# FFN front: first half of the tokens normalised in place and split first, four block products between the turns of the second half

## The chip, the cores and the metric

The kernel is one program on 1 core of a Trainium2 chip. The metric is device time in microseconds (us), median of several runs; one further execution was recorded by the hardware profiler.

## What is computed

One layer of an encoder trunk on 1024 tokens of width 1024 in float32: a half-step SwiGLU FFN, a mixer part (attention and a state space branch), a second half-step SwiGLU FFN, and a last RMSNorm. The change is in the FFN, which runs twice:

```python
h = h + FFN_RES * _swiglu(_rmsnorm(h, ffn1_norm[l]), ffn1_w_gate[l], ffn1_w_up[l], ffn1_w_down[l])
# _rmsnorm: x * lax.rsqrt(mean(x * x) + EPS) * g
# _swiglu:  (silu(x @ w_gate) * (x @ w_up)) @ w_down        D_MODEL 1024, D_FF 2816
```

## The kernel before

`ffn_phase` is called at L220 and L233 of the listing's builder (first FFN with `x` in DRAM, second FFN with the tokens already in the SBUF tensor `rows`). Its first part computes gate and up products as block products of the seven-product (Winograd) form. A "matrix" n is 256 columns of w_gate (n even) or w_up (n odd), 22 in all; its four 512x128 quarters A11..A22 and their sums S (four `sums(n)` instructions on POOL, L1109) are the stationary side, seven products q = 0..6 per matrix. The moving side B is the normalised tokens, turned to feature-by-token: seven blocks of 512 features by 512 tokens, q = 0 and 2 from the first 512 tokens alone (B11, B21), q = 6 from the second 512 alone (B22), q = 1, 3, 4, 5 from sums T of both. Each operand is split in a high and a low half (`hi` by ACT, `lo = src - hi` by DVE), and each product is 4 k-steps of three passes, 12 matmuls of 128x512 (L48 to L50).

The front, before the first product, does for pairs of token tiles i (tile i and tile i+4, 128 tokens each):

- SP loads the tiles of `x` (first FFN only), the gain `gb`, and w_gate's first matrix `raw0` (L780 to L786). The second FFN stores all of `rows` to DRAM in one transfer here (L788, 4 MB). w_up's first matrix `raw1` is loaded after the last turn (L789, L790).
- ACT squares each row (L844) with a sum, and takes the root (L379).
- DVE makes 1/sqrt with a five-step Newton chain (L92 to L96, 128x2 elements, each step waiting for the one before), and scales both tiles into a pair buffer (L961, `xn`, two buffers in turn).
- POOL makes the four sums T of the pair (L1092 to L1097), one buffer.
- PE turns the seven blocks of the pair, four 128x128 transposes each, into PSUM banks 0 to 6 (L1133). Block q of the next pair waits until DVE has read block q of the last (`s_blo`).
- ACT copies each bank to `B_hi` (L849), DVE subtracts it from the bank into `B_lo` (L968).

After four pairs the seven products of matrix 0 start, then matrix 1, and so on (`matrix`, L1141 to L1164). Per matrix the products go to three banks: product 0 to bank a, copied by ACT to `t1` (L879); product 1 to bank b, t2 = b + t1 by DVE (L1009); product 3 waits for t2; t3 after product 3 (L1016); then c22, c21, c12 (L1019 to L1024). ACT writes the next matrix's `A_hi` (L863) and DVE its `A_lo` (L944) for slot q once product q of the present matrix is done. At the start of an odd matrix ACT also applies Silu to three quarters of the gate result (L871), which needs product 6 of the matrix before. In the first FFN the engines carry a second job beside the products, the `Tables` of the state space branch, advanced by `tables_on(n, q)` in each slot: in slot (0,6) PE turns lam (L488) and ACT does an Exp (L524); in slots (1,0) and (1,2) PE turns c (L496), the second waiting for ACT's copy of the first (L530); in slot (1,0) DVE multiplies (L555).

The order on each engine is written by hand; the code of the front before:

```python
for i in range(QUAD):
    turn(i)
for j in range(2):
    matrix(0, j, True)
```

## Time and profile before

| what | value |
| --- | --- |
| median of 3 runs | 2445.79 us (2445.03 to 2451.75) |
| the profiled execution's own time | 2445.71 us |
| its span, first to last instruction | 2443.6 us |
| mean granted TensorE clock | 0.958 of full speed |
| PE, DVE, ACT, POOL busy | 91%, 52%, 35%, 24% of the span |
| front of the first FFN, to its first product | 0 to 58.22 us |
| front of the second FFN, rows complete to first product | 1721.9 to 1772.25 us |

Times inside the trace are microseconds from the span's start. An instruction's row has its start, its duration, engine, line, operation, written tile<-read tiles, shape and count; in square brackets the idle time of the engine before it and what ended it.

### The profile page before, as it was taken

What the parts mean: (1) busy time and instruction counts of PE and PEld (TensorE: products, weight loads), DVE (VectorE), ACT (ScalarE), POOL (GpSimd) and SP (SyncE); (2) the same over time, 40 slices, a digit from 0 to 9 for tenths busy, and PEclk for the clock granted to TensorE, in tenths of its full rate; (3) what the DMA queues carried; (4) which work ended last, traced back from release to release, by engine and by line L of the source; (5) the groups of instructions that cost most, each with busy time, mean ns of one, the idle gap of its engine ahead of it and who ended that gap; (6) DMA issues with size and microseconds to landing.
All of it is one profiled execution on the core that took longest, in us unless ns stands there. A gap on an engine that the chain in (4) does not pass through costs nothing. (4 is left out here: it accounts for less than half of the span.)

```text
span 2443.6 us, 27322 instructions
## 1 busy us (share of the span) xinstructions
PE 2227.4 (91%) x10338; PEld 1846.6 (76%) x10338; DVE 1281.9 (52%) x1944; ACT 863.9 (35%) x1396; POOL 582.6 (24%) x500
## 2 busy tenths in 40 slices
PE   3999999989996979998959998799599999999997
PEld 3878888878885878886837776577488888888886
DVE  7685555533435327952347777451755555543444
ACT  5423233322223233153137776321432323322232
POOL 4347777600000002220002221000533233310000
PEclk8999999999997999998979999899699999999999
DMA  2323232373112363322420000241222222246111
GB/s 100 101 91 102 89 112 97 101 285 103 48 35 93 114 104 131 102 78 71 127 73 6 4 6 1 95 177 39 95 87 92 81 87 69 90 182 224 50 53 67
DMA packets 169729, 223.63 MB, mean 92 GB/s; under 512 B 32064, under 2 KB 121664, under 8 KB 169088
## 3 DMA queue, kind: packets, MB, share of 16 engines
q1 hardware_dynamic: 169600, 221.90, 28.1%
q8 instruction: 83, 1.36, 0.2%
q14 instruction: 46, 0.38, 0.1%
HBM read 162.58 MB, written 59.28 MB: 91 GB/s over the span
## 5 line engine op out<-in xcount | busy, mean ns | idle before, releaser
L48 PE MATMUL psum<-f_B_hi,f_A_hi 128*128 128x512 f32 x1232 | 483.5, 392 | 1.4 <-ACT rows L879 1.1
L50 PE MATMUL psum<-f_B_hi,f_A_lo 128*128 128x512 f32 x1232 | 479.8, 389 | 0.0
L49 PE MATMUL psum<-f_B_lo,f_A_hi 128*128 128x512 f32 x1232 | 479.5, 389 | 0.0
L48 PE MATMUL psum<-f_wd_hi,f_hh 128*128 128x512 f32 x704 | 274.8, 390 | 8.0 <-DVE f_hh L979 8.0
L49 PE MATMUL psum<-f_wd_lo,f_hh 128*128 128x512 f32 x704 | 274.4, 390 | 0.0
L50 PE MATMUL psum<-f_wd_hi,f_hh 128*128 128x512 f32 x704 | 274.4, 390 | 0.0
L48 PEld LDWEIGHTS psum<-f_B_hi,f_A_hi 128*128 128x128 f32 x1232 | 231.3, 188 | 50.0 <-issue 2.8
L50 PEld LDWEIGHTS psum<-f_B_hi,f_A_lo 128*128 128x128 f32 x1232 | 231.2, 188 | 48.7
L49 PEld LDWEIGHTS psum<-f_B_lo,f_A_hi 128*128 128x128 f32 x1232 | 231.4, 188 | 46.9
L977 DVE TENSOR_TENSOR f_wd_lo<-f_wd_raw,f_wd_hi 128x1024 fp32r<-128x1024 f32 x88 | 107.8, 1225 | 301.0 <-ACT f_wd_hi L898 301.0
L898 ACT CAST f_wd_hi<-f_wd_raw 128x1024 fp32r<-128x1024 f32 x88 | 92.8, 1055 | 352.2 <-PE psum L50 324.1
L863 ACT CAST f_A_hi<-f_S 128x512 fp32r<-128x512 f32 x176 | 109.4, 623 | 302.6 <-PE psum L50 295.6
L1109 POOL TENSOR_TENSOR f_S<-f_raw 128x512 f32<-128x512 f32 x88 | 132.4, 1505 | 310.2 <-DVE f_A_lo L944 291.6
L944 DVE TENSOR_TENSOR f_A_lo<-f_raw,f_A_hi 128x512 fp32r<-128x512 f32 x128 | 125.1, 978 | 135.2 <-ACT f_A_hi L863 134.6
L48 PEld LDWEIGHTS psum<-f_wd_hi,f_hh 128*128 128x128 f32 x704 | 132.5, 188 | 36.3 <-issue 8.4
L50 PEld LDWEIGHTS psum<-f_wd_hi,f_hh 128*128 128x128 f32 x704 | 132.4, 188 | 27.9
L49 PEld LDWEIGHTS psum<-f_wd_lo,f_hh 128*128 128x128 f32 x704 | 132.6, 188 | 27.4
L863 ACT CAST f_A_hi<-f_raw 128x512 fp32r<-128x512 f32 x132 | 82.1, 622 | 143.9 <-PE psum L50 139.5
L944 DVE TENSOR_TENSOR f_A_lo<-f_S,f_A_hi 128x512 fp32r<-128x512 f32 x174 | 125.4, 722 | 8.4 <-ACT f_A_hi L863 7.4
L2004 DVE TENSOR_TENSOR at_PT_lo<-psum,at_PT_hi 128x512 fp32r<-128x512 f32 x128 | 87.8, 687 | 66.1 <-ACT at_PT_hi L1900 65.8
L1516 POOL TENSOR_TENSOR u<-u,ss_C_mat 128x512 f32<-128x512 f32 x8 | 9.8, 1271 | 426.9 <-DMA ss_C_mat<-ssm_d 426.9
L48 PE MATMUL psum<-nT_hi,ga_hi 128*128 128x512 f32 x256 | 100.0, 390 | 0.9 <-DVE u L1530 0.9
(306 smaller groups left out, 4064.0 us busy)
## 6 DMA issues: line engine op xcount, KB each, us to landing
f_raw<-ffn_w_gate SPq DMA_DIRECT2D x22, 1024.0 KB, 5.4
f_raw<-ffn_w_up SPq DMA_DIRECT2D x22, 1024.0 KB, 5.5
hidden<-rows SPq DMA_DIRECT2D x22, 1024.0 KB, 6.2
f_h_raw<-hidden SPq DMA_DIRECT2D x88, 256.0 KB, 2.7
f_wd_raw<-ffn_w_down SPq DMA_DIRECT2D x44, 512.0 KB, 14.3
rows<-x SPq DMA_DIRECT2D x16, 512.0 KB, 7.8
kept<-rows SPq DMA_DIRECT2D x2, 4096.0 KB, 15.0
ga_raw<-w_in SPq DMA_DIRECT2D x16, 512.0 KB, 4.5
```

Source lines behind the costliest of these rows:

```text
L48: pe.matmul(out, lhs_hi, rhs_hi, start=first, stop=False, skip_group_check=go_on)
L49: pe.matmul(out, lhs_hi, rhs_lo, start=False, stop=False, skip_group_check=go_on)
L50: return pe.matmul(out, lhs_lo, rhs_hi, start=False, stop=last, skip_group_check=go_on)
L863: act.copy(A_hi[:, q], src).then_inc(s_hi, 1)
L898: act.copy(wd[u % 2][0][:], wd_raw[u % FT][:]).then_inc(s_dhi, 1)
L944: eng.tensor_tensor(A_lo[:, q], src, A_hi[:, q].bitcast(F32), ALU.subtract).then_inc(s_lo, 1)
L977: dve.tensor_tensor(wd[u % 2][1][:], wd_raw[u % FT][:], wd[u % 2][0][:].bitcast(F32), ALU.subtract).then_inc(s_dlo, 1)
L1109: pool.tensor_tensor(S[:, i], a, b, op).then_inc(s_sum, 1)
L1516: pool.tensor_tensor(u[:, g], u[:, g], Db[:, g].unsqueeze(2).broadcast_to([P, 4, T, SG]), ALU.mult).then_inc(s["ud"], 1)
L2004: dve.tensor_tensor(pt(PT_lo, g, x), turned_bank(x), pt(PT_hi, g, x).bitcast(F32), ALU.subtract).then_inc(s["tr_lo"], 1)
```

## The change

It acts on the front and on matrices 0 and 1 of both FFNs; all later matrices keep their order.

- `scaled` normalises a tile in place in `rows`; the pair buffers `xn` are gone. In the second FFN the store of `rows` is now eight transfers, tile by tile, and the scaling of a tile waits for its own store.
- Tiles come in order 0 to 7. Tiles 0 to 3 (first 512 tokens) are normalised in two groups, and PE turns only their two blocks q = 0 and 2 (`turn_lows`), each tile into banks of its own. DVE and ACT split these and `A` of matrix 0's products 0 and 2.
- Then each of tiles 4 to 7 meets its partner: POOL's sums T, now in two buffers, and PE turns blocks 6, 4, 3, 1, 5 (`turn_sums`).
- Between these turns PE does four products: (matrix 0, product 0), (0,2), (1,0), (1,2). `matrix` then skips them, in slots where `tables_on` is still called. `t1` of matrix 0 has a place of its own.
- POOL does `sums(0)` first, then the four `combine`. The first three `A_lo` of matrix 0 were POOL's and are now DVE's, with those of matrix 1's products 0 and 2.
- `raw0` is now loaded between x tiles 3 and 4, `raw1` right after tile 7 and no longer after the turns.

The core of the diff:

```diff
+EARLY = ((0, 0), (0, 2), (1, 0), (1, 2), (0, 1), (0, 3), (0, 4), (0, 5), (0, 6), (1, 1), (1, 3), (1, 4), (1, 5), (1, 6))
+LOW_BLOCKS, LOW_BANKS = (0, 2), ((0, 1), (3, 4), (5, 6), (0, 1))
+SUM_BLOCKS = (6, 4, 3, 1, 5)
...
-        xn = [at(f"xn_{n}", [P, 2, D], F32, n, 6 * KB) for n in ("A_hi", "A_lo")]
-        dump, gb = at("dump", [P, D], F32, "A_lo"), at("gb", [P, D], F32, "ring")
-        T = at("T", [P, 4, HALF], F32, "raw", 8 * KB)
+        t1_first = at("t1_first", [P, HALF], F32, "ring", 4 * KB)
+        t1_of = lambda n: t1 if n else t1_first[:]
+
+        dump, gb = at("dump", [P, D], F32, "B_hi", 8 * KB), at("gb", [P, D], F32, "ring")
+        T = [at(f"T_{n}", [P, 4, HALF], F32, n, 6 * KB) for n in ("A_lo", "A_hi")]
...
+            def take(m):
+                if x is not None:
                     sp.dma_start(rows[:, m, :], x[m * P:(m + 1) * P, :]).then_inc(s_x[m], 16)
+                else:
+                    sp.dma_start(residual[m * P:(m + 1) * P, :], rows[:, m, :]).then_inc(s_kept[m], 16)
+            take(0)
+            take(1)
             sp.dma_start(gb[:], gain.rearrange("(a d) -> a d", a=1).broadcast_to([P, D])).then_inc(s_gain, 16)
-            if x is not None:
-                for pair in order[1:]:
-                    for m in pair:
-                        sp.dma_start(rows[:, m, :], x[m * P:(m + 1) * P, :]).then_inc(s_x[m], 16)
+            take(2)
+            take(3)
             load_matrix(0)
...
-            sp.wait_ge(s_tr, PRODUCTS * QUAD)
+            for m in range(QUAD, ST):
+                take(m)
             load_matrix(1)
+            sp.wait_ge(s_tr, ALL_TURNED)
...
+            def squares(i):
+                square(2 * i)
+                square(2 * i + 1)
+                norm.root(act, i, slice(2 * i, 2 * i + 2))
+
+            def lows_high(m):
+                for i, q in enumerate(LOW_BLOCKS):
+                    act.wait_ge(s_tr, low_turned(m, i))
+                    act.copy(B_hi[:, q, :, tile(m)], blocks(LOW_BANKS[m][i])).then_inc(s_bhi, 1)
...
+            def first_copy(j):
+                act.wait_ge(s_mm, place(j, 0) + 1)
+                act.copy(t1_of(j), bank(banks[j][0])).then_inc(s_t1, 1)
...
+            squares(0)
+            squares(1)
+            lows_high(0)
+            lows_high(1)
+            high(0, 0)
+            high(0, 2)
+            squares(2)
+            lows_high(2)
+            lows_high(3)
+            squares(3)
+            first_copy(0)
+            high(1, 0)
+            sums_high(0)
+            high(1, 2)
+            sums_high(1)
+            first_copy(1)
+            sums_high(2)
+            sums_high(3)
+            for q in (1, 3, 4, 5, 6):
...
+            def scaled(m):
+                if m == 0:
+                    dve.wait_ge(s_gain, 16)
+                if x is None:
+                    dve.wait_ge(s_kept[m], 16)
+                dve.scalar_tensor_tensor(out=rows[:, m, :], in0=rows[:, m, :], scalar=stat[:, 3, m:m + 1],
+                                         in1=gb[:], op0=ALU.mult, op1=ALU.mult).then_inc(s_xn, 1)
+
+            def normalised(i):
+                variance(i)
+                rstd(i)
+                scaled(2 * i)
+                scaled(2 * i + 1)
...
-            variance(0)
-            rstd(0)
-            scaled(0)
-            variance(1)
-            rstd(1)
-            scaled(1)
-            variance(2)
-            variance(3)
-            blocks_low(0)
-            rstd(2)
-            scaled(2)
-            blocks_low(1)
-            rstd(3)
-            scaled(3)
-            blocks_low(2)
-            blocks_low(3)
-            for q in range(3, PRODUCTS):
+            normalised(0)
+            normalised(1)
+            lows_low(0)
+            lows_low(1)
+            low(0, 0)
+            low(0, 2)
+            normalised(2)
+            lows_low(2)
+            lows_low(3)
+            normalised(3)
+            low(1, 0)
+            sums_low(0)
+            low(1, 2)
+            sums_low(1)
+            sums_low(2)
+            sums_low(3)
+            for q in (1, 3, 4, 5, 6):
...
+                lo_, hi_, t = rows[:, i, :], rows[:, QUAD + i, :], T[i % 2]
                 B11, B21, B12, B22 = lo_[:, 0:HALF], lo_[:, HALF:], hi_[:, 0:HALF], hi_[:, HALF:]
-                if i:
-                    pool.wait_ge(s_tr, PRODUCTS * i)
-                pool.wait_ge(s_xn, 2 * i + 2)
-                pool.tensor_tensor(T[:, 0], B12, B11, ALU.subtract).then_inc(s_T, 1)
-                pool.tensor_tensor(T[:, 2], B22, B12, ALU.subtract).then_inc(s_T, 1)
+                if i >= 2:
+                    pool.wait_ge(s_tr, sum_turned(i - 1, -1))
...
-            combine(0)
-            combine(1)
             sums(0)
-            combine(2)
-            for q in range(3):
-                low_half(pool, 0, q)
-            combine(3)
+            for i in range(QUAD):
+                combine(i)
...
+            def turn_lows(m):
+                pe.wait_ge(s_xn, m + 1)
+                if m == QUAD - 1:
+                    pe.wait_ge(s_blo, low_turned(0, LOWS - 1))
+                for i in range(LOWS):
+                    turn(LOW_BANKS[m][i], rows[:, m, i * HALF:(i + 1) * HALF])
+
+            def turn_sums(m):
+                t = T[m % 2]
+                ready = ((s_xn, QUAD + m + 1), (s_T, 4 * m + 1), (s_T, 4 * m + 2), (s_T, 4 * m + 3), (s_T, 4 * m + 4))
+                for i, src in enumerate((rows[:, QUAD + m, HALF:], t[:, 0], t[:, 2], t[:, 1], t[:, 3])):
+                    pe.wait_ge(*ready[i])
+                    if m:
+                        pe.wait_ge(s_blo, sum_turned(m - 1, i))
+                    turn(SUM_BLOCKS[i], src)
+
+            def first_product(j, q):
+                pe.wait_ge(s_lo, place(j, q) + 1)
+                if q == 0 and j == 0:
+                    pe.wait_ge(s_blo, LOWS * QUAD)
+                if q == 2:
+                    pe.wait_ge(s_t1, j + 1)
+                product(bank(banks[j][0]), q, q == 0, True)
...
+                    if first and q in LOW_BLOCKS:
+                        tables_on(n, q)
+                        continue
...
+            for m in range(QUAD):
+                turn_lows(m)
+            for m in range(QUAD):
+                first_product(*EARLY[m])
+                turn_sums(m)```

Three places of the engines' order follow, as lists of instructions in program order (`f_` stands for either FFN's tiles; `f_raw_73` is `raw0`, `f_raw_74` is `raw1`).

PE at the head of the FFN phase, the piece that stood there (first pair, then the start of matrix 0 after the fourth pair):

```order
L1133 MATMUL psum<-ident,f_xn_A_hi 128x128 x4
L1133 MATMUL psum<-ident,f_T 128x128 x4
L1133 MATMUL psum<-ident,f_xn_A_hi 128x128 x4
L1133 MATMUL psum<-ident,f_T 128x128 x12
L1133 MATMUL psum<-ident,f_xn_A_hi 128x128 x4
```

and the piece that stands there now (the three L48 to L50 rows are the first of four equal triples of product (0,0); the same pattern of one product and twenty transposes follows three times more):

```order
L1163 MATMUL psum<-ident,rows 128x128 x32
L48 MATMUL psum<-f_B_hi,f_A_hi 128x512
L49 MATMUL psum<-f_B_lo,f_A_hi 128x512
L50 MATMUL psum<-f_B_hi,f_A_lo 128x512
...
L1163 MATMUL psum<-ident,rows 128x128 x4
L1163 MATMUL psum<-ident,f_T_A_lo 128x128 x16
```

All 32 transposes of the first half's two blocks moved ahead of everything, and twelve matmuls of a product stand before each tile's twenty.

DVE between the second group's scaling and the split of the second half, before:

```order
L961 SCALAR_TENSOR_TENSOR f_xn_A_lo<-rows,f_stat,f_gb 128x1024 x2
L375 TENSOR_SCALAR f_stat<-f_stat 128x2 x2
L968 TENSOR_TENSOR f_B_lo<-psum,f_B_hi 128x4x128 x7
L92 RECIPROCAL f_stat<-f_stat 128x2
```

and now, from the same place to the last tile's split:

```order
L990 SCALAR_TENSOR_TENSOR rows<-rows,f_stat,f_gb 128x1024 x2
L1002 TENSOR_TENSOR f_B_lo<-psum,f_B_hi 128x4x128 x4
L974 TENSOR_TENSOR f_A_lo<-f_raw_73,f_A_hi 128x512 x2
...
L96 TENSOR_TENSOR f_stat<-f_stat 128x2
L990 SCALAR_TENSOR_TENSOR rows<-rows,f_stat,f_gb 128x1024 x2
L974 TENSOR_TENSOR f_A_lo<-f_raw_74,f_A_hi 128x512
L1007 TENSOR_TENSOR f_B_lo<-psum,f_B_hi 128x4x128 x5
L974 TENSOR_TENSOR f_A_lo<-f_raw_74,f_A_hi 128x512
L1007 TENSOR_TENSOR f_B_lo<-psum,f_B_hi 128x4x128 x15
```

DVE scales all four groups before it splits any block that needs a sum, and carries five `A_lo` in the front.

PE in the first FFN around the end of matrix 0: twelve rows of product (1,0) stood between the turns of lam and of c, and product (1,2) ahead of the second turn of c. Now, with the last matmul of (0,6) first and the first triple of (1,1):

```order
L50 MATMUL psum<-f_B_hi,f_A_lo 128x512
L488 MATMUL psum<-ident,tb_lam_raw 128x32 x2
L496 MATMUL psum<-ident,tb_c_raw 128x128 x4
L48 MATMUL psum<-f_B_hi,f_A_hi 128x512
...
L50 MATMUL psum<-f_B_hi,f_A_lo 128x512
L496 MATMUL psum<-ident,tb_c_raw 128x128 x4
```

One product, (1,1), is left between the two turns of c, and between the end of matrix 0 and product (1,3).

## Rows read from the trace of the kernel before

**Rows 1.** The page: span, then busy time and share of each engine
```profile
span 2443.6 us, 27322 instructions
...
PE 2227.4 (91%) x10338; PEld 1846.6 (76%) x10338; DVE 1281.9 (52%) x1944; ACT 863.9 (35%) x1396; POOL 582.6 (24%) x500
```

**Rows 2.** Stretches: us, busy (x instructions) by engine, PEclk, DMA share, GB/s
```profile
0.00:58.20 58.20, 20.14 (x112) 18.07 (x113) 41.15 (x58) 27.93 (x52) 30.31 (x29) 0.82 0.28 100
1715.00:1774.00 59.00, 30.14 (x144) 26.49 (x143) 48.22 (x69) 28.78 (x54) 31.51 (x23) 0.68 0.26 99
10.00:12.00 2.00, 0.00 (x0) 0.00 (x0) 0.00 (x0) 1.75 (x3) 0.00 (x0) 1.00 1.03 420
```

**Rows 3.** Waits of PE and of PEld, 0 to 60 us: total, times, longest
```profile
PEld psum L1133 <- DVE f_xn_A_hi L961: 22.9, 2, 16.4
...
PE psum L1133 <- DVE f_B_lo L968: 11.5, 3, 6.3
```

**Rows 4.** Timeline, ACT and DVE, 12.5 to 18 us
```profile
12.56 1.28 ACT L379 ACT_TABLE_LOAD   x1
...
15.09 2.48 DVE L961 SCALAR_TENSOR_TENSOR f_xn_A_hi<-rows,f_stat,f_gb 128x1024 f32<-128x1024 f32 x2
```

**Rows 5.** Timeline, DVE and POOL, 33 to 46 us
```profile
33.38 4.45 DVE L961 SCALAR_TENSOR_TENSOR f_xn_A_hi<-rows,f_stat,f_gb 128x1024 f32<-128x1024 f32 x2
...
42.13 0.94 DVE L93 TENSOR_TENSOR f_stat<-f_stat 128x2 f32<-128x2 f32 x1
...
43.01 1.27 POOL L944 TENSOR_TENSOR f_A_lo<-f_raw,f_A_hi 128x512 fp32r<-128x512 f32 x1
43.10 1.20 DVE L94 TENSOR_TENSOR f_stat<-f_stat 128x2 f32<-128x2 f32 x1
...
45.57 1.18 DVE L96 TENSOR_TENSOR f_stat<-f_stat 128x2 f32<-128x2 f32 x1
```

**Rows 6.** Timeline, runs of the splits, ACT then DVE
```profile
25.32 3.98 ACT L849 CAST f_B_hi<-psum 128x512 fp32r<-128x512 f32 x8
...
37.76 4.27 DVE L968 TENSOR_TENSOR f_B_lo<-psum,f_B_hi 128x512 fp32r<-128x512 f32 x7
```

**Rows 7.** Timeline, PE, second FFN, turns before and after an idle stretch
```profile
1740.92 0.68 PE L1133 MATMUL psum<-ident,f_xn_A_lo 128*128 128x128 f32 x4
1744.69 1.11 PE L1133 MATMUL psum<-ident,f_T 128*128 128x128 f32 x4 [3.09 <-POOL f_T L1095]
```

**Rows 8.** Timeline, PE: first matmuls of matrices 0 and 2, both FFNs
```profile
58.22 0.50 PE L48 MATMUL psum<-f_B_hi,f_A_hi 128*128 128x512 f32 x1
...
98.17 0.39 PE L48 MATMUL psum<-f_B_hi,f_A_hi 128*128 128x512 f32 x1
...
1772.25 0.47 PE L48 MATMUL psum<-f_B_hi,f_A_hi 128*128 128x512 f32 x1
...
1810.55 0.39 PE L48 MATMUL psum<-f_B_hi,f_A_hi 128*128 128x512 f32 x1
```

**Rows 9.** Timeline, first FFN, from the end of matrix 0
```profile
77.79 0.31 PE L488 MATMUL psum<-ident,tb_lam_raw 32*128 32x32 f32 x2
...
78.58 1.28 ACT L524 ACT_TABLE_LOAD   x1
...
79.88 0.23 ACT L524 ACTIVATE tb_sc<-tb_ldt 128x32 f32<-128x32 f32 x1
...
83.38 0.62 ACT L863 CAST f_A_hi<-f_raw 128x512 fp32r<-128x512 f32 x1
...
84.10 0.69 DVE L944 TENSOR_TENSOR f_A_lo<-f_raw,f_A_hi 128x512 fp32r<-128x512 f32 x1 [4.23 <-ACT f_A_hi L863]
...
85.59 0.69 DVE L1009 TENSOR_TENSOR rows<-psum,rows 128x512 f32<-128x512 f32 x1
```

**Rows 10.** Timeline, second FFN, the same place, ACT
```profile
1792.43 1.49 ACT L871 ACTIVATE rows<-rows 128x1536 f32<-128x1536 f32 x1
```

**Rows 11.** DMA issues of the first FFN's front: KB each, us to landing
```profile
f_raw<-ffn_w_gate SPq DMA_DIRECT2D x1, 1024.0 KB, 13.3
```

More of the change, by code:

```diff
@@ L752, in ffn_phase @@
         s_gain, s_sq, s_xn, s_T, s_tr, s_bhi, s_blo = map(sem, ("gain", "sq", "xn", "T", "tr", "bhi", "blo"))
-        s_kept = sem("kept")
+        s_kept = [sem(f"kept{m}") for m in range(ST if x is None else 0)]
         s_raw = [sem(f"raw_in{j}") for j in range(2)]
@@ L768, in ffn_phase @@
         block = ctx.enter_context(nc.Block())
-        order = [(i, i + QUAD) for i in range(QUAD)]
+        tile = lambda m: slice(m % QUAD * P, (m % QUAD + 1) * P)
+        LOWS, SUMS = len(LOW_BLOCKS), len(SUM_BLOCKS)
+        low_turned = lambda m, i: LOWS * m + i + 1
+        sum_turned = lambda m, i: LOWS * QUAD + SUMS * m + i + 1
+        ALL_TURNED = PRODUCTS * QUAD
+        place = lambda n, q: PRODUCTS * n + q if n >= 2 else EARLY.index((n, q))
         tile_banks = lambda i: psum[:, 2 * ((i + 3) % 4):2 * ((i + 3) % 4) + 2, :]
@@ L837, in _, with square, sums_high @@
         def _(act):
-            def square(i):
-                for j, m in enumerate(order[i]):
-                    if x is not None:
-                        act.wait_ge(s_x[m], 16)
-                    if i + j:
-                        act.wait_ge(s_sq, 2 * i + j)
-                    act.activation(dump[:], rows[:, m, :], ACT.Square, accum_out=stat[:, 0, 2 * i + j:2 * i + j + 1]).then_inc(s_sq, 1)
-            def blocks_high(i):
-                for q in range(PRODUCTS):
-                    act.wait_ge(s_tr, PRODUCTS * i + q + 1)
-                    act.copy(B_hi[:, q, :, i * P:(i + 1) * P], blocks(q)).then_inc(s_bhi, 1)
+            def square(m):
+                if x is not None:
+                    act.wait_ge(s_x[m], 16)
+                if m:
+                    act.wait_ge(s_sq, m)
+                act.activation(dump[:], rows[:, m, :], ACT.Square, accum_out=stat[:, 0, m:m + 1]).then_inc(s_sq, 1)
+            def squares(i):
[6 more added lines that the diff above has]
+                    act.copy(B_hi[:, q, :, tile(m)], blocks(LOW_BANKS[m][i])).then_inc(s_bhi, 1)
+            def sums_high(m):
+                if m == 0:
+                    act.wait_ge(s_sq, ST)
+                for i, q in enumerate(SUM_BLOCKS):
+                    act.wait_ge(s_tr, sum_turned(m, i))
+                    act.copy(B_hi[:, q, :, tile(m)], blocks(q)).then_inc(s_bhi, 1)
+            def first_copy(j):
+                act.wait_ge(s_mm, place(j, 0) + 1)
+                act.copy(t1_of(j), bank(banks[j][0])).then_inc(s_t1, 1)
             def high(n, q):
@@ L953, in variance, with lows_low, sums_low @@
                 norm.var(dve, i, slice(2 * i, 2 * i + 2))
[L955 to L968 removed]
+            def scaled(m):
+                if m == 0:
+                    dve.wait_ge(s_gain, 16)
[8 more added lines that the diff above has]
+                scaled(2 * i + 1)
+            def lows_low(m):
+                for i, q in enumerate(LOW_BLOCKS):
+                    dve.wait_ge(s_bhi, low_turned(m, i))
+                    dve.tensor_tensor(B_lo[:, q, :, tile(m)], blocks(LOW_BANKS[m][i]), B_hi[:, q, :, tile(m)].bitcast(F32), ALU.subtract).then_inc(s_blo, 1)
+            def sums_low(m):
+                for i, q in enumerate(SUM_BLOCKS):
+                    dve.wait_ge(s_bhi, sum_turned(m, i))
+                    dve.tensor_tensor(B_lo[:, q, :, tile(m)], blocks(q), B_hi[:, q, :, tile(m)].bitcast(F32), ALU.subtract).then_inc(s_blo, 1)
             def low(n, q):
@@ L1025, in matrix @@
                     if n + 1 < MATS:
-                        low(n + 1, q)
+                        if n or q not in LOW_BLOCKS:
+                            low(n + 1, q)
                     elif q == 4:
@@ L1182, in _ @@
             tables_on = beside(pe, "pe")
-            for i in range(QUAD):
-                turn(i)
+            for m in range(QUAD):
+                turn_lows(m)
+            for m in range(QUAD):
+                first_product(*EARLY[m])
+                turn_sums(m)
             for j in range(2):
```

89 lines of the change are left out of this document (27 added, 62 removed).

## The prediction

> **What bounds the kernel now.** The page comes first: the span is 2443.6 us and PE is busy for 91% of it [rows 1], so only places where PE idles can give much. The stretches by engine show two of them, the fronts of the two FFNs: up to 58.2 us PE is busy for 20.1 us while DVE is busy for 41.2, and from 1715 to 1774 for 30.1 against DVE's 48.2 [rows 2]. The waits of the first front say for whom: PE's weight loads stood for the scaled rows of DVE, the longest time 16.4 us, and its matmuls three times for DVE's splits of the last pair (11.5 us) [rows 3]. So a front is a chain through DVE, and POOL runs beside it. Once matrix 0 begins PE does not stop: 14 products from 1772.25 to 1810.55 are 2.74 us each, and the first FFN goes from 58.22 to 98.17 with its turns of lam and c between [rows 8]. The ends of the comparison are therefore the starts of matrix 2, 98.17 and 1810.55: what the change brings there it keeps.
>
> **DVE and POOL exclude each other.** This is the price that decides the new front. DVE's L93 on 128x2 elements took 0.94 us, L94 1.20 and L96 1.18, each ending as a POOL instruction ends; POOL's take 1.27 and start 1.22 apart. Two scalings beside POOL took 4.45 [rows 5], where two alone took 2.48 [rows 4]. So a Newton chain costs 1.0 us alone and 4 x 1.22 = 4.9 beside POOL. Splits out of PSUM pay nothing: seven in 4.27, 0.60 each; ACT's half is 0.50 each (eight in 3.98) [rows 6].
>
> **The new front, first FFN, step by step** (by hand, from those durations).
> - *First rows.* The table load stood behind four squares, at 12.56 [rows 4]; now it stands behind two, so the first scaling comes at about 10.4, not 15.09. The second group ends its squares when tile 3 has landed. Before, the data moved at 420 GB/s [rows 2]; ahead of raw0 stand four tiles and the gain, 2.6 MB, and its own 1 MB, so it lands at about 14 and no longer 13.3 us after an issue at 6.1 [rows 11]. At 14 POOL starts `sums(0)`, just when the second Newton chain runs: 13.8 + 4.9 + 2.45 = 21.2 for scaled tiles 2 and 3.
> - *To the first product.* Six subtractions (3.6), variance, root and Newton alone (1.4), two scalings (2.45), four splits (2.4): 31.0. PE has idled and starts at 1.2 GHz; that costs nothing, since DVE is still the longer path.
> - *Second half.* POOL now has eight sums in a row from 28.5, so the last Newton chain and both scalings collide: 0.6 + 4.9 + 4.5, then matrix 1's first `A_lo` (1.2 + 0.6), then five splits (3.0): 46.0. From there PE binds: the last turn of tile 5 (to 46.9), two products (5.5) and two times twenty transposes (4.3) make 56.9 with 0.2 of signals. Behind the last turn stand ACT's five casts, one `A_hi`, DVE's last split and `A_lo`, 3.0 us: product (0,1) starts at 59.9. Before, it was the second product, at 58.22 + 2.74 = 60.96. The front itself is hardly shorter, by 1.0 us; what is gained is that three further products are behind it, 8.2.
>
> **What matrices 0 and 1 give back.** Skipping products (0,2), (1,0) and (1,2) there takes away the cover of the sums that stood under them.
> - Product (0,3) waits for t2, which DVE makes after (0,1): 0.69 and the signals, 0.9 us. Product (0,2) covered it.
> - Product (1,3) waits for t2 of matrix 1. DVE makes it behind `A_lo` of (2,0), which waits for ACT's `A_hi`, which stands behind the Silu, which needs the end of matrix 0. In the trace matrix 0 ended at about 77.7, the `A_hi` came at 83.38, `A_lo` at 84.10 and t2 at 85.59 [rows 9]. The copy to t1 (0.5 us) leaves that chain and DVE's wait shrinks with it, so t2 ends some 8.0 us after matrix 0, while PE has one product and 0.65 us of small turns to do: 3.4. PE stands 4.6 us. Three products covered it before. The second turn of c, behind ACT's copy of the first, is ready 1 us earlier and hides in this wait.
> - In the second FFN there is no Exp and no table load: Silu at 1792.43 for 1.49 [rows 10], then `A_hi` 0.5, `A_lo` 0.7, t2 0.7: 4.1 after the end of matrix 0 against 2.74 of product, 1.4 us.
> - *Clock.* After 3.1 us idle the second FFN's turns went from 0.68 to 1.11 us for four, that is to the 1.2 GHz level [rows 7]. The new front has an idle stretch of 2.8 us before (0,1) and one of 4.6 before (1,3). A whole product at 1.2 GHz costs 2.7 more. Nearest rows say it may or may not fall; between 0 and 5.4 per FFN I take 1.3 in the first, 0.5 in the second, where the second stop is short.
>
> A rule weighed here: the Trainium skill, ScalarE: Activation LUTs, section "What ACT_TABLE_LOAD costs", puts a further drain of 1.38 us behind each load. The trace disagrees: the load at 78.58 took 1.28 and the Exp began at 79.88, 0.02 behind it [rows 9]. By the Trainium skill's figure, two loads would lengthen the 4.6 to 7.4; the row decides.
>
> **Sum, first FFN:** 1.0 + 8.2 - 0.9 - 4.6 - 1.3 = 2.4 us. **Second FFN:** the gain, third in SP's queue, and not the squares, lets the first scaling begin, at about 1727.8; the second Newton chain is then over before raw0 lands (1733.5), but `sums(0)` meets the first two `A_lo` (2.4 more). The first product comes at 1746.5, and by the same steps (28.9 us) product (0,1) at 1775.4, where 1775.0 was its time: 8.2 - 0.4 - 0.9 - 1.4 - 0.5 = 5.0 us. The eight stores cost nothing: each lands before its scaling, since tile 4's, some 14 us after SP's first issue, is needed after 20. SP's other edits cost nothing either; the reload of raw0 still stands behind the table DMAs, now 1 us earlier, and has 4 us in hand. DVE takes three `A_lo` from POOL (1.8 us), counted above. Together **7.4 us**.
>
> The same durations, applied to the old order, put the first products at 58.0 and 1772.6; the trace has 58.22 and 1772.25 [rows 8]. So the steps are good to about 0.5 us each, the order of collisions to some 2 us. The profiled execution took 2445.71 us, 2.1 beyond its span, and the median is 2445.79, so its sum carries over: 2445.8 - 7.4 = **2438.4 us**.
>
> **Rivals.**
> - *The collisions miss each other.* If raw0 lands after the second Newton chain, or DVE wins the race for single steps, a chain falls from 4.9 to 1.0. Half of the four collisions of both FFNs (3.9 + 3.9 + 3.9 + 2.4 = 14) give 7 us more: 2431. For: raw0's landing and the chain lie within 1 us of each other. Against: in the old front three of four chains collided. Beyond first product (1,0) PE binds too, so not all arrives. Chance 0.12.
> - *The gain is eaten.* ACT's chain behind matrix 0 grows (raw0's reload late for `sums(2)`, on which the second `A_hi` and then the turn of c wait), or both idle stretches cost a cold product in both FFNs: 7.4 - 5 = 2 us or less, 2443.5. For: the chain passes ACT, POOL and SP. Against: 4 us in hand. Chance 0.20.
> - *Slower: the clock stays at 1.2 GHz through the second half of the front.* Granted clock over the old fronts was 0.82 and 0.68 of full speed [rows 2], with PE turning in small pieces. If the pieces of 20 transposes and one product do not lift it, or it falls at every wait, then from 46 on PE runs two products and 40 transposes at half speed: +5.5 + 4.3, (0,1) +2.7 and (1,3) +1.4, 13.9 per FFN. 2438.4 + 27.8 = 2466. The kernel is slower than before once more than a quarter of that happens (7.4 of 27.8), and by over 0.3% from about half of it. Against: the old kernel's first product ran at 2.4 GHz behind a dense stretch of turns, and the new stretch is denser. Chance 0.08, with smaller mixtures of it.
> - *The forecast, 4 to 11 us gained:* 0.60.
>
> **How the numbers follow.** A measurement of this kernel tells about 0.3%, 7.3 us, from no change, and the forecast lies on that edge. Of its 0.60 I put 0.31 above and 0.29 below. Faster: 0.12 + 0.31 = 0.43; same: 0.29 + 0.20 less 0.01, with nothing from the slow case = 0.48; slower: 0.08 and 0.01 of the eaten gain, 0.09. The range takes half of the first rival and most of the second: 2432.5 to 2445.
>
> **What would show it.** In the new profile: first scaling at 10 to 11 us; first product at 31 (29 if the collision misses) and 1746.5; product (0,1) at 60 and 1775.4; PE idle 0.9 us before (0,3), and 4.6 and 1.4 before (1,3), ended by DVE's t2 (L1048); matrix 2 at 95.8 and 1805.5 (the second less the first FFN's gain). Newton steps of 1.2 us beside POOL show the collisions. It is wrong if PE stands at c's turn (L496) longer than at t2, if a tile's scaling waits for a store, or if the granted clock is 0.5 from 46 to 57.

## The result, and the profile of the changed kernel

The changed kernel takes 2434.23 us, median of 5 runs (2429.93 to 2440.66); the kernel before, beside it, 2446.03 (2445.03 to 2451.75). The ratio is 0.9948, with a 95% interval of [0.9926, 0.9969]: 11.8 us less, of a forecast 7.4. The profiled execution took 2434.23 us, 11.5 less than the one of before.

The page, span and PE:

```profile
span 2432.5 us, 27318 instructions
PE 2231.1 (92%) x10338; PEld 1848.2 (76%) x10338; DVE 1281.9 (53%) x1950; ACT 864.4 (36%) x1396; POOL 580.1 (24%) x494
```

The two fronts by engine, columns as in [rows 2]:

```profile
0.00:58.20 58.20, 34.09 (x168) 28.18 (x169) 45.05 (x69) 32.88 (x61) 32.99 (x28) 0.97 0.38 125
1715.00:1774.00 59.00, 35.16 (x175) 28.95 (x176) 47.47 (x71) 33.01 (x62) 34.43 (x24) 0.74 0.35 122
```

Up to 58.2 us PE is busy for 34.1 and no longer for 20.1 us, at a granted clock of 0.97 against 0.82 [rows 2]. The starts that answer to [rows 8], in PE's timeline: product (0,0), (0,1), (0,3), (1,3), (1,4) and matrix 2 of the first FFN, the last matmul of the phase ahead of the second FFN, and there (0,0), (0,1), (0,3), (1,3) and matrix 2:

```profile
28.80 0.77 PE L48 MATMUL psum<-f_B_hi,f_A_hi 128*128 128x512 f32 x1 [6.67 <-DVE f_B_lo L1002]
55.00 0.79 PE L48 MATMUL psum<-f_B_hi,f_A_hi 128*128 128x512 f32 x1 [2.64 <-DVE f_A_lo L974]
60.34 0.47 PE L48 MATMUL psum<-f_B_hi,f_A_hi 128*128 128x512 f32 x1 [0.93 <-DVE rows L1048]
79.56 0.77 PE L48 MATMUL psum<-f_B_hi,f_A_hi 128*128 128x512 f32 x1 [0.35 <-DVE rows L1048]
83.48 0.39 PE L48 MATMUL psum<-f_B_hi,f_A_hi 128*128 128x512 f32 x1
91.64 0.39 PE L48 MATMUL psum<-f_B_hi,f_A_hi 128*128 128x512 f32 x1
...
1713.43 0.39 PE L50 MATMUL psum<-wo_hi,mg_mT_lo 128*128 128x512 f32 x1
1741.53 0.76 PE L48 MATMUL psum<-f_B_hi,f_A_hi 128*128 128x512 f32 x1 [9.65 <-DVE f_B_lo L1002]
1767.71 0.50 PE L48 MATMUL psum<-f_B_hi,f_A_hi 128*128 128x512 f32 x1 [2.64 <-DVE f_A_lo L974]
1773.26 0.47 PE L48 MATMUL psum<-f_B_hi,f_A_hi 128*128 128x512 f32 x1 [0.93 <-DVE rows L1048]
1788.72 0.47 PE L48 MATMUL psum<-f_B_hi,f_A_hi 128*128 128x512 f32 x1 [1.59 <-DVE rows L1048]
1799.71 0.39 PE L48 MATMUL psum<-f_B_hi,f_A_hi 128*128 128x512 f32 x1
```

Matrix 2 of the first FFN starts 6.5 us earlier (98.17 before). In the second FFN it starts 86.3 us behind the last matmul of the merge phase, where before it was 90.6 (1810.55 less 1719.94): 4.3 us. Together 10.9 of the 11.1 us by which the spans differ. What became of the expected stops is in PE's waits, 0 to 110 us (total, times, longest):

```profile
PE psum L1163 <- DVE rows L990: 13.0, 2, 11.8
PE psum L48 <- DVE f_B_lo L1002: 6.7, 1, 6.7
PE psum L496 <- ACT tb_C L530: 3.2, 1, 3.2
PE psum L48 <- DVE f_A_lo L974: 2.6, 1, 2.6
PE psum L1163 <- DVE f_B_lo L1002: 1.5, 1, 1.5
PE psum L48 <- DVE rows L1048: 1.3, 2, 0.9
```

**Where the forecast's front went.** DVE's timeline around the second Newton chain, and below it POOL's, at its first sum:

```profile
13.30 0.17 DVE L92 RECIPROCAL f_stat<-f_stat 128x2 f32<-128x2 f32 x1 [0.27 <-ACT f_stat L379]
13.50 0.16 DVE L93 TENSOR_TENSOR f_stat<-f_stat 128x2 f32<-128x2 f32 x1
...
14.09 0.16 DVE L96 TENSOR_TENSOR f_stat<-f_stat 128x2 f32<-128x2 f32 x1
14.29 4.56 DVE L990 SCALAR_TENSOR_TENSOR rows<-rows,f_stat,f_gb 128x1024 f32<-128x1024 f32 x2
```

```profile
14.28 1.27 POOL L1149 TENSOR_TENSOR f_S<-f_raw 128x512 f32<-128x512 f32 x1 [12.80 <-DMA f_raw<-ffn_w_gate]
```

The chain ended at 14.25 and POOL began at 14.28: it missed the collision that the sum had priced by 0.03 us, and only the two scalings paid (4.56 instead of 2.48). The miss is no accident of one execution: in all ten profiled executions of this first front without an added wait (those of the experiments below included) the chain took 0.95 or 0.96 us and the first product came at 28.65 to 28.81. In two of them (again, two_a01) POOL began up to 0.07 us before the chain's end, when its last step was already running.

**The first wait of the second front.** DVE's first scaling in the second FFN:

```profile
1722.58 2.48 DVE L990 SCALAR_TENSOR_TENSOR rows<-rows,f_stat,f_gb 128x1024 f32<-128x1024 f32 x2 [2.35 <-DMA f_gb<-ffn_norm]
```

Its Newton chain was over at 1720.22, and it stood 2.35 us for the gain. SP issues the gain behind the stores of tiles 0 and 1 (512 KB each) now, 3.1 us behind the merge phase's last matmul, and it lands 6.0 us later; before, it was the first issue, 1.9 us behind that matmul, and landed after 4.8. In the kernel before it thus landed 6.7 us behind that matmul, which would be 1720.2 here, so most of the wait comes from the new order of SP's queue. No run puts the gain back in front; what that would bring stays open.

### The profile page after: what moved, and what is told of

Same layout as the page of the kernel before. It is cut to its first block and busy times, and to the rows that moved or that the text cites. A ratio compares the mean times of both kernels' runs of the same rounds, so it can differ in the third digit from the quotient of the medians.

```text
span 2432.5 us, 27318 instructions
## 1 busy us (share of the span) xinstructions
PE 2231.1 (92%) x10338; PEld 1848.2 (76%) x10338; DVE 1281.9 (53%) x1950; ACT 864.4 (36%) x1396; POOL 580.1 (24%) x494
## 5 line engine op out<-in xcount | busy, mean ns | idle before, releaser
L48 PE MATMUL psum<-f_B_hi,f_A_hi 128*128 128x512 f32 x1232 | 488.0, 396 | 26.8 <-DVE f_B_lo L1002 16.3
L50 PE MATMUL psum<-f_B_hi,f_A_lo 128*128 128x512 f32 x1232 | 483.3, 392 | 0.0
L49 PE MATMUL psum<-f_B_lo,f_A_hi 128*128 128x512 f32 x1232 | 483.1, 392 | 0.0
L48 PEld LDWEIGHTS psum<-f_B_hi,f_A_hi 128*128 128x128 f32 x1232 | 233.5, 189 | 78.1 <-issue 22.7
L48 PE MATMUL psum<-f_wd_hi,f_hh 128*128 128x512 f32 x704 | 275.1, 391 | 8.5 <-DVE f_hh L1018 8.5
L50 PE MATMUL psum<-f_wd_hi,f_hh 128*128 128x512 f32 x704 | 274.8, 390 | 0.0
L49 PE MATMUL psum<-f_wd_lo,f_hh 128*128 128x512 f32 x704 | 274.8, 390 | 0.0
L50 PEld LDWEIGHTS psum<-f_B_hi,f_A_lo 128*128 128x128 f32 x1232 | 233.4, 189 | 49.4
L49 PEld LDWEIGHTS psum<-f_B_lo,f_A_hi 128*128 128x128 f32 x1232 | 233.6, 190 | 47.2
L1149 POOL TENSOR_TENSOR f_S<-f_raw 128x512 f32<-128x512 f32 x88 | 133.1, 1513 | 481.3 <-DVE f_A_lo L974 299.0
L889 ACT CAST f_A_hi<-f_S 128x512 fp32r<-128x512 f32 x176 | 109.5, 625 | 310.4 <-PE psum L50 306.5
L974 DVE TENSOR_TENSOR f_A_lo<-f_raw,f_A_hi 128x512 fp32r<-128x512 f32 x132 | 132.1, 1002 | 126.2 <-ACT f_A_hi L889 125.6
L48 PEld LDWEIGHTS psum<-f_wd_hi,f_hh 128*128 128x128 f32 x704 | 132.9, 189 | 36.3 <-issue 8.9
L49 PEld LDWEIGHTS psum<-f_wd_lo,f_hh 128*128 128x128 f32 x704 | 132.9, 189 | 27.8
L50 PEld LDWEIGHTS psum<-f_wd_hi,f_hh 128*128 128x128 f32 x704 | 132.7, 189 | 27.6
L889 ACT CAST f_A_hi<-f_raw 128x512 fp32r<-128x512 f32 x132 | 82.1, 623 | 140.0 <-PE psum L50 138.9
L974 DVE TENSOR_TENSOR f_A_lo<-f_S,f_A_hi 128x512 fp32r<-128x512 f32 x176 | 128.5, 732 | 5.7 <-ACT f_A_hi L889 4.3
L48 PE MATMUL psum<-nT_hi,ga_hi 128*128 128x512 f32 x256 | 100.0, 390 | 0.9 <-DVE u L1590 0.9
## 6 DMA issues: line engine op xcount, KB each, us to landing
f_raw<-ffn_w_gate SPq DMA_DIRECT2D x22, 1024.0 KB, 5.4
f_raw<-ffn_w_up SPq DMA_DIRECT2D x22, 1024.0 KB, 5.5
hidden<-rows SPq DMA_DIRECT2D x22, 1024.0 KB, 6.3
```

The costliest lines, as they stand in the source:

```text
L48: pe.matmul(out, lhs_hi, rhs_hi, start=first, stop=False, skip_group_check=go_on)
L49: pe.matmul(out, lhs_hi, rhs_lo, start=False, stop=False, skip_group_check=go_on)
L50: return pe.matmul(out, lhs_lo, rhs_hi, start=False, stop=last, skip_group_check=go_on)
L889: act.copy(A_hi[:, q], src).then_inc(s_hi, 1)
L974: eng.tensor_tensor(A_lo[:, q], src, A_hi[:, q].bitcast(F32), ALU.subtract).then_inc(s_lo, 1)
L1149: pool.tensor_tensor(S[:, i], a, b, op).then_inc(s_sum, 1)
```

## The experiments

All are timed against the kernel before on the same chip. Between the two FFNs the code is the same in all of them, yet in the profiled executions the stretch from matrix 2 of the first FFN (of before: 98.17) to the merge phase's last matmul (1719.94) took from 1617.3 (a01_early) to 1627.6 us (held). So besides the medians the runs are read by two marks that leave this stretch out: **F1**, where matrix 2 of the first FFN starts, and **F2**, how long behind the merge phase's last matmul it starts in the second. Each mark is of one execution. The same code gave an F1 of 91.64, 90.88 and 92.26 (changed, again, f1_only), since the clock took different amounts from products (0,1) and (1,3), and an F2 of 86.28, 86.23 and 86.40.

| kernel | median, us (runs) | before beside it | ratio, 95% | F1 | F2 |
| --- | --- | --- | --- | --- | --- |
| before | 2446.03 (5) | | | 98.17 | 90.61 |
| changed | 2434.23 (5) | 2446.03 | 0.9948 [0.9926, 0.9969] | 91.64 | 86.28 |
| again | 2431.42 (5) | 2446.04 | 0.9938 [0.9926, 0.9951] | 90.88 | 86.23 |
| f1_only | 2437.64 (6) | 2445.11 | 0.9972 [0.9959, 0.9985] | 92.26 | 90.33 |
| f2_only | 2439.84 (11) | 2445.11 | 0.9981 [0.9971, 0.9991] | 98.73 | 86.40 |
| forced | 2441.26 (12) | 2445.11 | 0.9990 [0.9979, 1.0001] | 95.30 | 91.42 |
| held | 2436.80 (6) | 2445.11 | 0.9964 [0.9951, 0.9977] | 93.91 | 86.37 |
| warm | 2435.45 (5) | 2445.80 | 0.9954 [0.9940, 0.9967] | 91.68 | 85.15 |
| t2_first | 2431.45 (5) | 2445.80 | 0.9948 [0.9935, 0.9961] | 91.23 | 85.87 |
| t2_silu | 2427.62 (5) | 2445.80 | 0.9930 [0.9916, 0.9943] | 86.88 | 85.18 |
| a01_early | 2427.33 (5) | 2445.80 | 0.9931 [0.9918, 0.9943] | 91.18 | 84.22 |
| both | 2428.30 (6) | 2446.04 | 0.9929 [0.9908, 0.9951] | 88.39 | 83.50 |
| two_early | 2433.46 (6) | 2446.04 | 0.9939 [0.9924, 0.9953] | 88.79 | 86.40 |
| two_a01 | 2433.19 (5) | 2445.06 | 0.9950 [0.9936, 0.9963] | 88.59 | 88.23 |

(One of warm's five runs took 11110.85 us; it is left out of its ratio.)

### One front at a time

f1_only gives the first FFN the new front and leaves the second FFN the function of before, f2_only the other way round:

```diff
-        ffn_phase(nc, "f2", w["ffn2_norm"][0], ...
+        ffn_phase_before(nc, "f2", w["ffn2_norm"][0], ...
```

> The first FFN has the new front, the second the old one. My account from the two traces (6.5 us came in the first FFN, 4.4 in the second): matrix 2 of the first FFN starts at about 91.6 us and the time is 6.5 us under before, near 2439.5. Rival (the forecast's split, 2.4 and 5.0): 2443.5. Rival (something of the gain lies outside the two fronts): the second FFN's start of matrix 2, counted from the completed rows, is not the one of before.

> The second FFN has the new front, the first the old one. My account: 4.4 us under before, near 2441.5; the two gains add up to the whole. Rival (the forecast's split): 5.0 under. If the two single changes add up to clearly more or less than 11 us, the fronts act on each other or on what lies between.

The medians are 7.5 and 5.3 us under before; F1 of f1_only is 5.9 under, F2 of f2_only 4.2. So each front brings alone what it brings in the changed kernel, to within 0.6 us, and the two medians add up to 12.7 where the changed kernel's is 11.8 under before: nothing of size lies elsewhere. By its ratio the interval of f1_only (3.7 to 10.0 us) excludes the forecast's 2.4; the forecast's 5.0 for the second FFN stands.

### Is it the collision? forced and held

```diff
                 variance(i)
+                if i == 1:
+                    dve.wait_ge(s_raw[0], 16)
                 rstd(i)
```

> The changed kernel with one wait more: DVE does not start the second Newton chain before raw0 has landed, so that it runs beside POOL's sums(0), as the forecast had it. Theory (the mis-sized term is this collision): the chain takes 4 steps of 1.2 us and some, the first product of the first FFN comes near 31 to 32 us and no longer at 28.8, matrix 2 up to 3 us later than 91.6, and the median is 1 to 4 us over the changed kernel's. Rival (the front is bound by PE and POOL from the first product on, so the early collision does not count): matrix 2 within 0.7 us of 91.6.

Timeline of DVE in forced, the same chain, and below it PE's, product (0,0) and matrix 2 of the first FFN:

```profile
14.49 0.17 DVE L92 RECIPROCAL f_stat<-f_stat 128x2 f32<-128x2 f32 x1 [1.44 <-DMA f_raw<-ffn_w_gate]
14.69 1.13 DVE L93 TENSOR_TENSOR f_stat<-f_stat 128x2 f32<-128x2 f32 x1
15.86 0.16 DVE L94 TENSOR_TENSOR f_stat<-f_stat 128x2 f32<-128x2 f32 x1
16.05 1.13 DVE L95 TENSOR_SCALAR f_stat<-f_stat 128x2 f32<-128x2 f32 x1
17.22 1.18 DVE L96 TENSOR_TENSOR f_stat<-f_stat 128x2 f32<-128x2 f32 x1
18.43 3.45 DVE L990 SCALAR_TENSOR_TENSOR rows<-rows,f_stat,f_gb 128x1024 f32<-128x1024 f32 x2
```

```profile
31.84 0.77 PE L48 MATMUL psum<-f_B_hi,f_A_hi 128*128 128x512 f32 x1 [6.93 <-DVE f_B_lo L1004]
95.30 0.39 PE L48 MATMUL psum<-f_B_hi,f_A_hi 128*128 128x512 f32 x1
```

With the collision the chain takes 3.9 us (14.49 to 18.40; the forecast had 4.9, but L94 slipped in between two POOL instructions) instead of 0.95, the first product comes at 31.84 (forecast: 31.0), and the 3.0 us reach the end of the first FFN's front: F1 is 3.7 later. The forecast's theory held, and the rival that the early collision doesn't count fell. But the 3.0 are not the price of the collision alone: 1.2 are the added wait (1.44 us idle before L92 instead of 0.27), 3.0 the longer chain, and the scalings behind it gave 1.1 back (3.45 instead of 4.56). By these rows a collision without the wait would cost some 1.9, an estimate. In the medians the kernel is 7.0 us over the changed one and not 1 to 4, because the edit acts on the second FFN too. There, in the changed kernel, the chain was over (1725.41 to 1726.36) before raw0 landed at 1729.2, and the wait put it behind: DVE stood 4.23 us for raw0, then collided, and F2 is 5.1 later. I had priced the edit in the first FFN only.

held has POOL wait until tiles 2 and 3 are scaled:

```diff
+            pool.wait_ge(s_xn, 4)
             sums(0)
```

> The changed kernel with POOL's sums(0) held back until tiles 2 and 3 are scaled: no Newton step or scaling of the second group can meet it, but the splits of A for products (0,0) and (0,2) may. Theory (the collision is hit in some executions of the changed kernel and missed in others, which is why its five times spread over 10.7 us, while those of before spread over 6.7): the spread falls to some 4 us, the pair of scalings takes 2.5 and not 4.56, the first product comes at 27 to 28.5, median 0 to 3 us under the changed kernel's. Rival (the spread has another source): the spread stays.

The scalings took 2.48, but the collision moved to the two `A_lo` (2.64 instead of 1.28) and the next variance (1.22 instead of 0.16), and the first product came at 29.20, later than without the wait. Nothing is gained, and the range of its times (8.9 us) is hardly smaller. The spread isn't this race: again, the changed kernel once more, spread over 2.8 us only, over 24 runs the kernel before spread over 12.9, and the race went the same way in all ten executions above.

> The changed kernel once more, beside the others on the same chip. The changed kernel's fronts have fixed lengths: matrix 2 within 1 us of 91.64, and 86.28 behind the phase before in the second FFN; what the whole differs by from execution to execution (some 10 us) lies between the two FFNs, where the code is that of before.

Its fronts are those of the changed kernel to 0.8 and 0.05 us.

### The stop before (1,3)

t2_first moves t2 of matrix 1 ahead of `A_lo` of (2,0); t2_silu also moves the Silu behind slot (1,2):

```diff
                     if q == 1:
                         dve.wait_ge(s_t1, n + 1)
+                        if n == 1:
+                            dve.wait_ge(s_c12, 1)
                         dve.tensor_tensor(t2, bank(b), t1_of(n), ALU.add).then_inc(s_t2, 1)
+                        if n == 1:
+                            low(2, 0)
...
-                        if n or q not in LOW_BLOCKS:
+                        if (n or q not in LOW_BLOCKS) and (n, q) != (1, 0):
                             low(n + 1, q)
```

> The changed kernel with DVE making t2 of matrix 1 ahead of A_lo of (2,0), so that t2 no longer stands behind ACT's Silu. Forecast's theory (the stop before (1,3) is the chain Silu, A_hi, A_lo, t2): that stop shrinks from 3.6 us to 0.9 in the first FFN, 2.7 and 1.2 of clock gained, and from 1.59 to 0.9 in the second: 4.6 us in all. Rival (after the trace: in the first FFN PE stands at c's second turn, for ACT's copy of the first, which is behind the Silu as well): the stop of 3.2 us before that turn stays, only the 0.35 us at t2 goes, 1.0 us in all.

> t2_first, and ACT's Silu of the three quarters of the first gate result moved behind slot (1,2). Rival of the last run: ACT's copy of c comes right after product (1,1), the turn at about 76.1 and (1,3) at 76.8 instead of 79.56, the clock does not fall there (1.2 us), 3.9 us in the first FFN, 0.65 in the second: 4.5 us under the changed kernel. Forecast's theory: the same as t2_first.

In t2_first PE's 3.2 us before c's second turn stayed (`PE psum L496 <- ACT tb_C L530: 3.2, 1, 3.2`), only the last 0.35 went. The reason is on ACT, whose timeline in the changed kernel reads:

```profile
71.57 0.62 ACT L889 CAST f_A_hi<-f_S 128x512 fp32r<-128x512 f32 x1 [2.10 <-PE psum L50]
72.21 1.28 ACT L524 ACT_TABLE_LOAD   x1
73.50 0.23 ACT L524 ACTIVATE tb_sc<-tb_ldt 128x32 f32<-128x32 f32 x1
73.64 0.20 ACT L526 COPY tb_lam<-psum 128x64 f32<-128x64 f32 x1
73.85 1.28 ACT L897 ACT_TABLE_LOAD   x1
75.15 1.48 ACT L897 ACTIVATE rows<-rows 128x1536 f32<-128x1536 f32 x1
76.54 0.60 ACT L889 CAST f_A_hi<-f_raw 128x512 fp32r<-128x512 f32 x1
77.05 0.61 ACT L889 CAST f_A_hi<-f_S 128x512 fp32r<-128x512 f32 x1
77.56 0.59 ACT L530 ACTIVATE tb_C<-psum 128x512 f32<-128x512 f32 x1
```

and in t2_silu, where the copy of c (L530) no longer stands behind a table load and the Silu:

```profile
73.88 0.62 ACT L889 CAST f_A_hi<-f_S 128x512 fp32r<-128x512 f32 x1 [0.81 <-PE psum L50]
74.41 0.59 ACT L530 ACTIVATE tb_C<-psum 128x512 f32<-128x512 f32 x1
74.90 0.61 ACT L889 CAST f_A_hi<-f_raw 128x512 fp32r<-128x512 f32 x1
75.53 1.28 ACT L897 ACT_TABLE_LOAD   x1
76.82 1.49 ACT L897 ACTIVATE rows<-rows 128x1536 f32<-128x1536 f32 x1
```

The stop went from 3.2 and 0.35 to 1.34 us, the clock didn't fall behind it, and F1 is 86.88: 4.8 us earlier than in the changed kernel, of which 1.25 are in product (0,1), which kept its clock here (below). t2_first shows that taking t2 from behind `A_lo` doesn't do alone. Whether moving the Silu alone would do isn't shown: no run does only that.

### The stop before (0,1), and the clock

warm fills a part of the stop before (0,1) with transposes of the identity, 1.1 us of it stay; a01_early takes its cause away:

```diff
+            for _ in range(14):
+                pe.transpose(psum[:, GATE_BANKS[1], 0:P], ident[:], ident[:])
             for j in range(2):
                 matrix(0, j, True)
```

```diff
             first_copy(1)
+            high(0, 1)
             sums_high(2)
             sums_high(3)
-            for q in (1, 3, 4, 5, 6):
+            for q in (3, 4, 5, 6):
                 high(0, q)
```

(the same for `low` on DVE, ahead of `sums_low(2)`)

> The changed kernel with 14 transposes of the identity into a free bank between the last turn and product (0,1), where TensorE stood 2.64 us. Theory (the stop lets the clock fall, so that product (0,1) takes 4.4 to 4.6 us and not 2.74): the product starts as before at about 55.0 and the next, (0,3), at 58.7 to 59 and not 60.34; the same in the second FFN; median 3.4 us under the changed kernel's. Rival (the slow product has another cause, such as the first matmul's operands): no change of the product, median the same or 0.3 over.

> The changed kernel with the high and low half of A for product (0,1) made before the splits of tiles 6 and 7, so that behind the last turn there are only casts and splits of B. Theory (the 2.64 us stop is ACT's five casts, then A_hi, then DVE's A_lo in a row, and it costs once more by the clock): the stop shrinks to about 1.0 us, product (0,1) starts at 53.4, takes 2.8 to 3 us at 2.4 GHz, 3.4 us per FFN: 6.8 in all. Rival (DVE's splits, with the A_lo between them and POOL's sums beside, are late instead): product (0,1) within 0.5 us of 55.0, no gain.

Granted clock (the third number from the end of each row) from 55 to 60 and from 78 to 84 us, in the changed kernel:

```profile
55.00:60.00 5.00, 4.41 (x12) 3.23 (x12) 3.94 (x5) 1.09 (x3) 3.56 (x3) 0.70 0.79 106
...
78.00:84.00 6.00, 5.35 (x19) 4.16 (x20) 3.95 (x12) 0.94 (x3) 0.00 (x0) 0.72 0.04 11
```

and in warm:

```profile
55.00:60.00 5.00, 3.82 (x16) 2.87 (x17) 3.90 (x5) 1.09 (x3) 3.71 (x3) 1.00 0.82 114
...
78.00:84.00 6.00, 5.82 (x16) 4.62 (x16) 2.79 (x8) 0.29 (x1) 0.00 (x0) 0.55 0.00 0
```

Product (0,1), started at 54.85, was followed by (0,3) at 59.05, 1.3 us earlier than in the changed kernel: with its stop of 1.18 it took 3.0 us and not 4.4. The second FFN's (0,1) took 3.0 too, where 4.6 stood. So the fall of the clock is real and can be kept off. Product (1,3) still began 1.3 us earlier (78.26 for 79.56). But behind the stop of 3.2 us before c's turn the clock now stayed low for longer (0.55 against 0.72), (1,3) took 5.3 us instead of 3.9, and F1 was 91.68: all of it gone. That the one follows from the other isn't shown: again, whose (0,1) took 3.0 too, has 4.3 there, and held, whose (0,1) took 4.6, has 5.3. In the second FFN, which has no such stop, 1.1 us stayed.

a01_early shows the same: (0,1) starts at 53.79, 0.4 later than expected, and keeps its clock, and (0,3) comes 1.9 us earlier, its own stop having grown from 0.93 to 1.71 since (0,1) now ends while DVE is still at the four `A_lo` that stand ahead of t2. (1,3) began 1.8 us earlier and took 5.3 us as well: F1 is 91.18, 0.5 us gained; F2 gained 2.1. Its median, 18.5 us under before, is more than its marks explain (7.0 + 6.4 = 13.4): its profiled execution also had the shortest stretch between the FFNs of all. I can't tell whether that is more than chance.

### Both, and fewer early products

both puts t2_silu and a01_early together; two_early leaves (1,0) and (1,2) in matrix 1, and two_a01 adds a01_early's edit to that:

```diff
-                first_product(*EARLY[m])
+                if m < 2:
+                    first_product(*EARLY[m])
                 turn_sums(m)
...
-                    if first and q in LOW_BLOCKS:
+                    if n == 0 and q in LOW_BLOCKS:
```

(ACT's and DVE's halves of these two products, and the copy to t1, move with them)

> t2_silu and a01_early in one kernel. If the stops they remove are separate, matrix 2 of the first FFN starts at 86.3 us (86.88 in t2_silu, where product (0,1) had kept its clock; a01_early's (0,3) came 0.6 earlier than that), and in the second FFN 83.1 us behind the last matmul of the phase before (86.28 in the changed kernel, less 1.10 and 2.06): 8.5 us under the changed kernel. Rival (what one stop gives up, the next takes, as in a01_early, where 1.9 us were gone again behind the stop before (1,3)): 87 or more, no better than t2_silu.

> The changed kernel with only products (0,0) and (0,2) between the turns; (1,0) and (1,2) stand in matrix 1 again, each with its A and the copy to t1. Theory (the two products are only partly hidden in the front, and in matrix 1 they cover the stops before c's turn and (1,3)): (0,1) starts near 51.5 us and no longer at 55.0, nothing stops behind matrix 0, matrix 2 starts near 89, 2.7 us earlier than the changed kernel; in the second FFN, where the stop before (1,3) is 1.6 us only, no gain, or a loss of up to 1.5. Rival (two products moved are 5.4 us gained): matrix 2 at 95 or later and the time 3 us or more over the changed kernel.

> two_early with a01_early's edit: the A of product (0,1) is made ahead of the splits of tiles 6 and 7. In two_early (0,1) stood 2.00 us and then took 5.5 us at the clock's lower level, and no stop of over 1 us is left behind it. Theory (stop and clock are both due to A_hi and A_lo standing last): (0,1) starts near 49.9 and takes 3 to 4.5 us, matrix 2 at 85 to 87 in the first FFN and 83 to 84.5 behind the phase before in the second; 5 to 8 us under the changed kernel, as good as t2_silu or both with half the early products. Rival (the clock falls because the turns of tiles 6 and 7 wait for POOL piece by piece): (0,1) still takes 5 us or more, and only the 1 us of the stop is gained in each FFN.

both has the best sum of marks with t2_silu (171.9 and 172.1, against 177.9 in the changed kernel and 188.8 before), but not the 169.4 expected: in its first FFN the clock fell at (1,3), behind stops of 1.34 and 0.58 us (75.79 to 80.21 for one product). It is no faster than t2_silu in the medians.

two_early asks what two of the four early products are worth. PE's timeline, products (0,1) and (0,3), matrix 2 of the first FFN and of the second:

```profile
50.97 0.80 PE L48 MATMUL psum<-f_B_hi,f_A_hi 128*128 128x512 f32 x1 [2.00 <-DVE f_A_lo L970]
57.34 0.47 PE L48 MATMUL psum<-f_B_hi,f_A_hi 128*128 128x512 f32 x1 [0.88 <-DVE rows L1042]
88.79 0.39 PE L48 MATMUL psum<-f_B_hi,f_A_hi 128*128 128x512 f32 x1
...
1801.93 0.39 PE L48 MATMUL psum<-f_B_hi,f_A_hi 128*128 128x512 f32 x1
```

With two of the four products back in matrix 1, F1 is 88.79, as expected, 2.1 to 3.5 us **earlier** than with all four (changed, again, f1_only), and F2 is 86.40, the same. So those two early products, 5.4 us of PE's work, brought nothing in the second FFN and cost 2 us or more in the first: PE reached (0,1) 4.0 us later, and behind matrix 0 it stood 3.6 us for ACT and DVE, which the two products would have covered. In the medians (2433.46 against 2431.42 and 2434.23) this can't be seen. It holds for the order as the change made it. With the stops taken away, all four early are better: t2_silu and both, which keep the four, have sums of marks of 172.1 and 171.9, two_early 175.2.

In two_a01 the stop before (0,1) went (49.59), but the one before (0,3) became 3.19 us, since DVE made t2 behind five `A_lo`, the last two of them, beside POOL, in 1.78 and 1.75 us. The product started where the theory has it and took 4.3 us, in its range, but F1 is unchanged, not 85 to 87, and F2 1.8 us worse. Its rival, that only the 1 us of the stop is gained, isn't right either; the stop moved.

## Why the prediction came out as it did

The direction and the range held: 2434.23 in 2432.5 to 2445.0, forecast 2438.4. The split did not: 2.4 and 5.0 us forecast, 6.5 and 4.3 measured. The first FFN's 2.4 was too low because product (0,1) came 4.9 us earlier than forecast, and the second's is near by errors that act against each other. By its own steps:

- **Bound by DVE's chain, POOL excluding it; gain at the start of matrix 2**: right up to the first product, and both fronts' gains add up to the whole, shown by f1_only and f2_only. Behind the first product PE bound, and not from 46 on: between 28.80 and 52.36 it idled 0.25 us.
- **First scaling at 10.4**: 10.46. **Second FFN**: first product forecast 26.6 us behind the merge phase (1746.5 less 1719.94), measured 28.1, because the gain vector landed 1.3 us later than assumed; product (0,1) forecast at 55.5, measured 54.3. What was won is 4.3 and not 5.0: against those 1.2 us, the stop forecast as 1.4 is 1.6, and (0,1) took 1.9 more than 2.74 where 0.5 stood for the clock.
- **The step that failed: "13.8 + 4.9 + 2.45 = 21.2 for scaled tiles 2 and 3".** The chain ran free, 0.95 us, and the collision fell on the scalings instead (4.56 for 2.45): tiles 2 and 3 were scaled at 18.85 and the first product came at 28.80, 2.2 us before the forecast's 31.0. With the hit forced it came at 31.84, 1.2 us of that by the wait. That is the rival "the collisions miss each other", for which I had named the right reason (raw0 lands within 1 us of the chain) and given 0.12. Where two events are forecast 0.2 us apart from steps good to 0.5, the chance of a miss is nearer a half.
- **The last chain was over-priced too**: 4.9 forecast, 3.5 measured in the changed kernel (29.01 to 32.47) and in forced (32.04 to 35.51): L94 slipped through and L93 waited half. Of the 4.9 us by which product (0,1) came earlier than forecast (55.0 for 59.9), 2.2 stood at the first product already, this is 1.4, and the stop before (0,1) is 0.4 (2.64 for 3.0); the rest is in smaller steps.
- **Give-backs 6.8 us in the first FFN**: measured 7.65 from (0,1) on, namely 0.93 before (0,3) (forecast 0.9), 1.67 by which (0,1) took longer than 2.74 (1.4 by the clock: between two stops it takes 3.0 at 2.4 GHz too, as in warm), 3.57 of stops before (1,3) (forecast 4.6), 1.48 by the clock in c's turn and (1,3) (both clock terms together forecast as 1.3). The stop was put down to t2; t2_first showed that c's turn, which I had "ready 1 us earlier", binds, by a chain through the same Silu. PE standing longer at c's turn (3.2 us) than at t2 (0.35) was one of the forecast's own signs of being wrong: there the stop's size was about right and its path was not.
- **"Three further products behind it, 8.2"**: as arithmetic right, but two_early shows that, with the stops as they are, only one of the three paid. The term was counted whole against the other terms, though the stops in matrices 0 and 1 exist only because these products were taken from there.
- **Eight stores and SP's order "cost nothing"**: no scaling waited for its own store, as said, but the first two stores stand ahead of the gain, and DVE stood 2.35 us for it. The forecast counted the gain's place in the queue and set its landing 1.3 us too early.

The Trainium skill's SBUF — State Buffer, section "Who interferes with whom", says that a DVE instruction with two SBUF inputs contends with a GpSimd instruction that reads SBUF, and one with at most one SBUF input outside the 2-port modes doesn't. The rows agree: beside POOL the reciprocal, one input, took 0.17 (at 29.01 in the changed kernel, within a POOL sum from 28.58 to 29.86), and L93 and L96 of forced, with two inputs, 1.13 and 1.18. L95, a tensor_scalar with one input, took 1.13 as well, which by that page puts this 128x2 float32 instruction into a 2-port mode.
